# A hybrid decoder step: split first loads, an early sigmoid table, lower parts moved to VectorE, and a reordered tail

## What is computed

```
z = x @ w_in                        # A: RG-LRU, B: conformer conv, C: pooling, D: short conv, and 4 gates
y_a = rg_lru(conv4(a_x)) * gelu(a_gate);  y_b = silu(LN(conv31(b_val * sigmoid(b_gate))))
y_c = pool(c_in) @ pool_w;                y_d = d_b * conv3(d_c * d_h)
merged = sum_n sigmoid(gate_n) * (y_n @ w_branch[n])
x = LN(alpha*x + merged @ w_out);  x = LN(alpha*x + (silu(x@w_g) * (x@w_u)) @ w_d)
```

## Time and profile before

| | |
|---|---|
| median of 3 runs | 941.07 us (940.93 to 941.18) |
| profiled execution: time / span | 940.77 / 939.0 us |
| TensorE busy | 922.2 us (98%) |
| VectorE, ScalarE, GpSimd busy | 704.4, 415.4, 325.8 us |
| HBM read / written | 89.94 / 7.62 MB |

### The profile page before, as it was taken

One profiled execution on the slowest core, in us unless ns is written; L12 is line 12 of the kernel. 1 busy time (PEld: TensorE's weight loads), 2 busy tenths in 40 slices (PEclk: granted clock), 3 DMA queues, 4 the chain that ended last, 5 costly groups with the idle time before them and its releaser, 6 DMA issues.

```text
span 939.0 us, 18699 instructions
## 1 busy us (share of the span) xinstructions
PE 922.2 (98%) x7311; PEld 918.6 (98%) x7311; DVE 704.4 (75%) x1032; ACT 415.4 (44%) x659; POOL 325.8 (35%) x260
## 2 busy tenths in 40 slices
PE   8999999999999999999999999999999999999995
PEld 8999999999999999999999999999999999999995
DVE  2799999899896898777777699888887878321125
ACT  4422232326657423545444357555554557222222
POOL 5765665658634453000006443000000004443324
PEclk9999999999999999999999999999999999999998
DMA  8633233322445623332433320443334333422202
GB/s 239 189 91 90 77 98 90 89 68 84 138 147 187 195 70 112 113 99 72 121 101 112 86 74 26 122 122 91 89 91 119 102 89 102 146 85 84 80 1 96
DMA packets 169109, 98.30 MB, mean 105 GB/s; under 512 B 4906, under 2 KB 164946, under 8 KB 169057
## 3 DMA queue, kind: packets, MB, share of 16 engines
q1 hardware_dynamic: 166825, 96.66, 35.4%
q10 hardware_dynamic: 2232, 0.92, 0.4%
HBM read 89.94 MB, written 7.62 MB: 104 GB/s over the span
## 4 chain that ended last, share of the span: by engine, by line
PE 91%; DVE 5%; POOL 2%; issue 1%; ACT 1%; DMA 0%; POOLq 0%; DVEq 0%
PE main L1274 48%; PE main L1426 26%; PE aux L1426 4%; PE aux L1274 4%; PE main L1498 3%; PE main L1688 1%; PE aux L1260 1%; POOL x_lo L720 1%; PE main L1307 1%; PE aux L1498 1%; DVE merged L2150 1%; DVE main L2147 0%; POOL w_lo L634 0%; DVE aux L2182 0%; DVE merged L2195 0%
## 5 line engine op out<-in xcount | busy, mean ns | idle before, releaser
L634 POOL TENSOR_TENSOR w_lo<-raw,w_hi 128x1024 fp32r<-128x1024 f32 (+1 forms) x100 | 231.4, 2318 | 566.6 <-ACT w_hi L757 566.0
L757 ACT ACTIVATE w_hi<-raw 128x1024 fp32r<-128x1024 f32 x128 | 135.1, 1057 | 152.9 <-PE main L1274 118.6
L1274 PE MATMUL main<-x_hi,w_lo 128*128 128x272 f32 x784 | 162.5, 288 | 1.0 <-ACT sig L874 1.0
L1274 PE MATMUL main<-x_hi,w_hi 128*128 128x272 f32 x784 | 162.2, 288 | 0.0
L1274 PE MATMUL main<-x_lo,w_hi 128*128 128x272 f32 x784 | 161.7, 288 | 0.0
L1274 PEld LDWEIGHTS main<-x_hi,w_lo 128*128 128x128 f32 x784 | 123.2, 188 | 1.3 <-ACT sig L874 1.3
L1274 PEld LDWEIGHTS main<-x_lo,w_hi 128*128 128x128 f32 x784 | 123.1, 188 | 0.0
L1274 PEld LDWEIGHTS main<-x_hi,w_hi 128*128 128x128 f32 x784 | 122.4, 189 | 0.0
L1808 DVE SCALAR_TENSOR_TENSOR aux<-glu_pad,miscT,aux 128x512 f32<-128x512 f32 x112 | 75.2, 748 | 0.0
L2135 DVE SCALAR_TENSOR_TENSOR scr<-x_lo,main 128x544 f32<-128x544 f32 x6 | 4.3, 722 | 86.9 <-PE main L1274 86.9
L1274 PE MATMUL main<-y,w_hi 128*128 128x272 f32 x400 | 66.2, 287 | 0.0
(11 more groups left out here) (423 smaller groups left out, 2602.6 us busy)
## 6 DMA issues: line engine op xcount, KB each, us to landing
raw<-in_w_in SPq DMA_DIRECT2D x64, 512.0 KB, 4.2
raw<-in_w_ff_gate SPq DMA_DIRECT2D x22, 512.0 KB, 4.0
raw<-in_w_ff_up SPq DMA_DIRECT2D x22, 512.0 KB, 5.0
raw<-in_w_branch SPq DMA_DIRECT2D x32, 256.0 KB, 3.4
raw<-in_w_ff_down SPq DMA_DIRECT2D x16, 512.0 KB, 3.7
raw<-in_w_out SPq DMA_DIRECT2D x8, 512.0 KB, 3.6
raw<-in_w_ff_down SPq DMA_DIRECT2D x8, 384.0 KB, 3.3
kept_sums<-g_made_hi SPq DMA_DIRECT2D x4, 544.0 KB, 3.8
```

Source lines behind the costliest of these rows:

```text
L634: pool.tensor_tensor(w_lo[s][:, 0:n, :], raw[s][:, 0:n, :], w_hi[s][:, 0:n, :].bitcast(F32), ALU.subtract).then_inc(w_lo_ready, 1)
L757: act.activation(w_hi[s][:, :, :], raw[s][:, :, :], ACT.Copy).then_inc(w_hi_ready, 1)
L1274: mm = pe.matmul(ps[:, h, :], w[s][:, k, :], x[:, h * HALF:(h + 1) * HALF], start=(first and k == 0 and j == 0), stop=(last and k == n - 1 ...
```

## The change

Head: x tile 0 is loaded ahead of the first weight tile, which comes in two halves, one behind x tile 0 and one behind x tile 1. ScalarE makes the upper part of the first half, VectorE that of the second, ahead of x's lower parts; GpSimd both lower parts, half by half. The second weight tile's upper part is made behind all of x's, its lower part by VectorE. Eight of the 14 idle transposes run ahead of the sample rows. `turn_x(2)` moves behind the first four chunks of the first unit. Table: a sigmoid of one column is put behind the exponential; `lambda_parts` moves ahead of the first round. Feed-forward: VectorE makes lower parts 4 to 7 of half 1; silu of the first tile and its product move ahead of one upper part and one sum. Tail: `last_statistics` and `finish` are cut in two, and the parts take another order.

```diff
 # SyncE
-            unit(0, 0, in_col(0, 0))
             for j in range(SEQ // P):
                 sp.dma_start(x_tok[:, j, :], x_p[:, j, :]).then_inc(x_landed[j], 16)
+                if j < 2:
+                    half = slice(j * (KD // 2), (j + 1) * (KD // 2))
+                    sp.dma_start(raw[0][:, half, :], in_col(0, 0)[:, half, :])\
+                      .then_inc((first_landed, raw_landed[0])[j], 16)
 # GpSimd
-            for u in range(RING):
+            first = slice(0, KD // 2)
+            pool.wait_ge(first_hi_ready, 1)
+            pool.tensor_tensor(w_lo[0][:, first, :], raw[0][:, first, :], w_hi[0][:, first, :].bitcast(F32),
+                               ALU.subtract).then_inc(first_lo_ready, 1)
+            rest = slice(KD // 2, KD)
+            pool.wait_ge(w_hi_ready, 1)
+            pool.tensor_tensor(w_lo[0][:, rest, :], raw[0][:, rest, :], w_hi[0][:, rest, :].bitcast(F32),
+                               ALU.subtract).then_inc(w_lo_ready, 1)
+            pool.wait_ge(w_lo_ready, 2)
+            for u in range(2, RING):
                 lo(u, u, 8)
...
-            for k in range(KD):
+            for k in range(KD // 2):
                 x1_lo(1, k)
 # ScalarE
-            hi(0, 0)
+            act.wait_ge(first_landed, 16)
+            act.activation(w_hi[0][:, 0:KD // 2, :], raw[0][:, 0:KD // 2, :], ACT.Copy).then_inc(first_hi_ready, 1)
...
-                if h == 0:
-                    hi(1, 1)
+            act.wait_ge(w_hi_ready, 1)
+            hi(1, 1)
             hi(2, 2)
...
             act.activation(spv[:, 1, :], spv[:, 0, :], ACT.Exp).then_inc(z_ready, 1)
+            act.activation(bn_rs[:, 1:2, 0:1], ones[:, 0:1], ACT.Sigmoid)
             pairs(0, 0, tails=True)
...
             x_sum_high(1)
-            x_sum_high(2)
             act.wait_ge(unit_done, U_FF + 1)
             act.activation(halves(S[0][:, :]), slot(0), ACT.Silu).then_inc(tile_out[0], 1)
             left_high(0, 0)
+            x_sum_high(2)
             x_sum_high(3)
 # TensorE
             pe.wait_ge(ident_ready, 1)
+            for _ in range(8):
+                pe.transpose(aux[:, 1, 0:P], ident[:, :], ident[:, :])
             pe.wait_ge(x_landed[4], 16)
...
-            for _ in range(14):
+            for _ in range(6):
...
+                    pe.wait_ge(*((first_lo_ready, 1) if k < KD // 2 else (w_lo_ready, 1)))
...
-            for j in range(3):
-                turn_x(j)
-            pe.wait_ge(w_lo_ready, 1)
+            turn_x(0)
+            turn_x(1)
             first_unit(0, range(0, KD // 2))
+            turn_x(2)
             turn_x(3)
 # VectorE
+            ve.wait_ge(raw_landed[0], 16)
+            ve.tensor_copy(w_hi[0][:, KD // 2:KD, :], raw[0][:, KD // 2:KD, :]).then_inc(w_hi_ready, 1)
...
+            ve.wait_ge(w_hi_ready, 2)
+            ve.wait_ge(w_lo_ready, 1)
+            ve.tensor_tensor(w_lo[1][:, :, :], raw[1][:, :, :], w_hi[1][:, :, :].bitcast(F32), ALU.subtract)\
+              .then_inc(w_lo_ready, 1)
...
+            lambda_parts()
             for c in range(KW):
...
-                if c == KW - 1:
-                    lambda_parts()
...
             last_sum(0, 0)
-            ve.wait_ge(affine_ready, KD + KH)
+            ve.wait_ge(x1_lo_ready, KD + KD // 2)
+            for k in range(KD // 2, KD):
+                cols = slice(HALF, NT)
+                ve.wait_ge(x1_hi_ready, KD + k + 1)
+                ve.tensor_tensor(x_lo[:, k, cols], merged[:, k, cols], x_hi[:, k, cols].bitcast(F32),
+                                 ALU.subtract).then_inc(x1_lo_ready, 1)
+            ve.wait_ge(affine_ready, 2 * KD)
...
             sum_x(2, a12, x_sum[:, 1, :, :], ALU.subtract)
+            ff_product(0, slot(1))
+            left_low(0, 0)
             sum_x(3, a11, a21, ALU.subtract)
             sum_low(0, 0, 2)
             sum_x_low(1)
-            ff_product(0, slot(1))
-            left_low(0, 0)
...
             last_statistics(0, 2, NTILE + 1)
+            last_scale(0, 2, NTILE + 1)
             ve.wait_ge(vecs_copied, 2)
+            weigh(rs_tok[:, :], B * T, NTILE, slice(0, D))
             finish(rs_tok[:, :], B * T, NTILE, slice(0, D))
+            weigh(r_tok[:, 2, left], P, 2, left)
+            residual_last(1)
             finish(r_tok[:, 2, left], P, 2, left)
-            residual_last(1)
             last_statistics(1, 0, 2)
+            ve.wait_ge(bn_var, 2)
+            weigh(r_tok[:, 0, left], P, 0, left)
+            last_scale(1, 0, 2)
+            right = slice(D // 2, D)
+            weigh(r_tok[:, 0, right], P, 0, right)
             finish(r_tok[:, 0, :], P, 0, slice(0, D))
+            weigh(r_tok[:, 1, left], P, 1, left)
             finish(r_tok[:, 1, left], P, 1, left)
```

More of the change, by code:

```diff
@@ L361, in build @@
         w_hi_ready, w_lo_ready = sem("w_hi_ready"), sem("w_lo_ready")
+        first_landed, first_hi_ready, first_lo_ready = map(
+            sem, ("first_landed", "first_hi_ready", "first_lo_ready"))
         unit_done = sem("unit_done")
@@ L2351, in _ @@
             sum_low(0, 0, 1)
-            ve.wait_ge(affine_ready, 2 * KD)
             ve.wait_ge(x_sum_ready, 2)
             sum_x(2, a12, x_sum[:, 1, :, :], ALU.subtract)
+            ff_product(0, slot(1))
+            left_low(0, 0)
             sum_x(3, a11, a21, ALU.subtract)
@@ L2435, in last_statistics, with last_scale @@
                 ins.then_inc(bn_var, 1)
+            def last_scale(h, j0, j1):
                 ve.wait_ge(bn_std, h + 1)
@@ L2440, in last_statistics, with weigh, finish @@
                 ve.wait_ge(bn_scale, h + 1)
-            def finish(t, q, j, cols):
+            def weigh(t, q, j, cols):
                 after(link(ve.scalar_tensor_tensor(t, t, bn_mv[0:q, j, 0:1], g_ps[0:q, cols],
                                                    ALU.subtract, ALU.mult)))
+            def finish(t, q, j, cols):
                 ve.scalar_tensor_tensor(t, t, bn_rs[0:q, j, 0:1], b_ps[0:q, cols], ALU.mult, ALU.add)\
```

## The result

| | before | after |
|---|---|---|
| median of the runs | 941.18 us (8 runs, 940.93 to 941.30) | 945.07 us (8 runs, 943.21 to 946.82) |
| profiled execution: time / span | 940.77 / 939.0 us | 944.89 / 943.1 us |
| TensorE, VectorE, GpSimd busy | 922.2, 704.4, 325.8 us | 924.1, 709.6, 317.3 us |

The changed kernel is slower: ratio 1.0042, interval 1.0031 to 1.0053, some 3.9 us, where 937.8 us was forecast. Its runs also lie 3.6 us apart, those of before 0.4.

The account below looks back on a forecast made before the run. TensorE, busy 922.2 of 939.0 us, was taken to bound the kernel until its last matmul. Gains of 0.8 + 1.0 + 1.3 + 0.2 = 3.3 us gave 937.8 us against the 941.07 median, range 936.7 to 939.2.

Parts of the forecast that it names:

- Sigmoid table: ScalarE near 218 us: dummy sigmoid moves the table load behind the exponential, ending TensorE's wait; 1.0 us gained (0.7 to 1.15).
- Head: Start of the kernel: first matmul moves from 11.27 to about 9.7, of which 0.8 us stays; bounds 0 and 1.3.
- slower rival: TensorE's clock falls in a new idle piece; by the head, up to 6.8 us more, 944.6 us; chance 0.03.
- Feed-forward entry: Near 570 us: TensorE's waits for GpSimd go, 2.1 us, less a new 0.8 us wait for an addition; net 1.3.
- short lengths: VectorE at the feed-forward entry: four operations stretched beside GpSimd return to short length, 2.3 us; rival that they stay, 0.08.
- still covered: First feed-forward quad: weights ready about 576.2, quad starts 578.3; the moved sum makes them 1.2 us later, still in time.
- Tail: After the last matmul: last store issued when it was, only tile 0's store starts earlier; 0.2 us gained, 0 to 0.5.

Follow-up runs that it names:

- table_only: The kernel before with the table part alone (dummy sigmoid behind the exponential, lambda_parts ahead of the first round): 943.72 us, ratio 1.0028 to before.
- stats_first: The changed kernel with VectorE's two statistics reads (b_mean, b_std) ahead of the addition g_sum(2, 0, 1): 941.35 us, ratio 1.0005 to before.
- all_but_table: The changed kernel with the sigmoid table part undone: 948.80 us, ratio 1.0073 to before.
- ff_only: The kernel before with the change's feed-forward entry alone: 940.32 us, ratio 0.9991 to before.
- tail_only: The kernel before with the change's tail alone: 941.87 us, ratio 1.0012 to before.
- no_head: The kernel before with the change's sigmoid table and feed-forward entry, statistics ahead of g_sum(2, 0, 1) and g_low(0) ahead of softplus: 939.36 us, ratio 0.9982 to before.

## Why the prediction was wrong

- **The failed step** is in its first paragraph: "nothing else of TensorE's waits comes near them. So a microsecond won early arrives at the end, as long as nothing else is late by then." A wait of 3.15 us appeared at 263 us with 1.6 us of clock behind it. I read the stage only up to 220 us, because the change ends there. The cover of 0.57 us of `b_std` and the distance of 0.39 us between VectorE and GpSimd at 258 us were both in the trace of before; with 1.8 us won ahead of them, both had to be priced. The runs agree: with the two reads ahead of the addition (stats_first) the wait is gone and the kernel takes 3.7 us less.
- **Sigmoid table**, forecast 1.0: TensorE's idle 1.02 us of the earlier trace rows went entirely, the load had left the path and no copy brought it back. 1.27 us with the restart of the matmuls, which I had not counted; that is above my bound of 1.15. Right at its place, in table_only too.
- **Head**, forecast 0.8, first matmul at 9.7: it came at 10.02 after (9.70 to 10.54 in the executions profiled), 0.53 us won, 1.16 lost in the worst. The mis-sized term is x tile 1: it was to be there at 7.7, and TensorE could turn it from 8.06 (after) to 8.44 (all_but_table), once without a gap (stats_first, first matmul at 9.70). That an idle piece could leave TensorE at its low level I had under the slower rival, and excluded since 1.02 us had once been survived. That row stands in a stretch of steady matmuls; here transposes at the low level come before the piece, and the clock has yet to rise. The early transposes did raise the clock sooner where no long piece followed.
- **Feed-forward entry**, forecast 1.3 as 2.1 less 0.8: 2.07 and 1.35, net 0.72. The short lengths came back as I said (the sum takes 1.29 us, at 573.69), and VectorE's stream was 0.4 us ahead as worked out (the addition at 594.55, less the 3.92 us by which TensorE was late there, is 590.63 against 591.00 of the earlier trace rows). Mis-sized was the wait: I looked only at the addition, and three products ahead of it hang on ScalarE's copies, which VectorE's stream makes late. Moving one sum behind the product I called "still covered"; it was so for the weights, not for the copy behind it on ScalarE.
- **Tail**, forecast 0.2: 0.9 lost. The step that failed is that GpSimd works without a gap "on rows that the change leaves alone". Its last rows come from ScalarE, and ScalarE waits for VectorE's scale; in the new order a multiplication of 0.75 us stands ahead of the reciprocal and the scale falls behind GpSimd's start.
- **The slower rival** had the right kind of mechanism and nearly the number (944.6), but not the place; the number is an accident. Its point of decision, an idle piece longer than 1.02 us, fits the gates only in part: five waits above it were followed by the low level, two were not. Its 0.03 was far too low, since I asked only about idle pieces in the parts that change.

The scatter fits: the runs of after mix the head's lottery (up to 1.7 us) and the clock behind the gates (0.1 to 2.8 us in the executions profiled). That the two together make all of it is argued, not shown. What decides a clock that falls after 2.44 us in one kernel and stays up after 3.17 in another was not found. Nor is it settled what makes VectorE's chain late in the first place. One suspect shows in the traces: among ScalarE's nine issues of stores at 221 to 229 us, mostly 0.3 to 0.45 us each, one takes 1.1 to 1.9 us in every kernel that has the head or is table_only. In after:

```profile
222.19 1.48 ACTq L872 DMA_DIRECT2D out_sample_pool<-st_s  x1
```

None does in before, ff_only, tail_only and no_head. Against TensorE's next gate unit, ScalarE's sigmoid behind the stores is then 0.9 us late in after, and its squares, and with them GpSimd's sums beside the softplus, 0.5 us. It wasn't tried by itself. In no_head GpSimd was first at 258 us (by 0.03 us) without such an issue, but there `g_low(0)` stands ahead of the softplus, which moves VectorE too; so that does not rule the suspect out.

## What to carry to other kernels

Winning time on the bound engine moves it against all others, so ahead of the forecast look through the rest of the kernel for the smallest cover: reads that end just in time, and pairs of VectorE and GpSimd instructions on SBUF that start within half a microsecond of each other. Put the instruction that frees another engine's buffer ahead of the one that can be shut out, even if the order looks free. An idle piece that is new in a warm-up is filled with idle work, and a kernel whose runs lie wide apart has a race or a clock in it that the profiled execution may not show.

## What the hardware showed that I had not expected

- 0.03 us decide over 2.2: the same addition takes 1.29 us when it starts first and 3.50 when GpSimd does, and the loser waits for the other's end.
- Operations on four columns or fewer are shut out alike: the softplus steps on four columns take 0.16 to 0.18 us alone and 1.0 to 1.4 us (one 2.3, one 0.44) beside GpSimd, seven of fifteen before and nine after, and the scale in the tail takes 1.21. Reads whose input is the accumulators are not (0.72 us beside a GpSimd operation of 2.40).
- TensorE's clock fell after a wait of 2.44 to 3.21 us in five executions of seven and not in the other two (2.43 and 3.17 us). It was low for 3.4 us in four of the five and for 6.8 us in all_but_table. In the head an idle piece of 0.60 us between transposes was followed by the low level, and one of 0.72 us was not.
- Before is not quite free of it: of its 35 runs beside the last four kernels one took 944.50 us and two took 942.47 and 942.64, and of the 25 beside the four ahead of them one took 944.08. Whether this is the same race was not seen, since none of them was profiled.
